# A decoder block on one core: small tables placed ahead of the large buffers in SBUF, so that the large ones start at multiples of 256 bytes

## The reference

```python
mod = c @ w_mod + b_mod;  shift, scale, gate = split(mod, 3)
u = x * (1.0 + scale) + shift
q, k, v, z_a, cb, cc, cx, z_b, g_a, g_b = split(u @ w_in)   # 8 x 1024, 2 x 2048 columns
o = rms_norm(diff_attention(rope(q), rope(k), v, lam)) * subln_gain * 0.8   # 8 heads
y_a = o * silu(z_a)
y_b = cb * causal_conv3(cc * cx, conv_w) * silu(z_b)
h = sigmoid(g_a) * (y_a @ w_proj_a) + sigmoid(g_b) * (y_b @ w_proj_b)
r = 2 ** 0.25 * x + gate * (h @ w_out)
y = layer_norm(r) * ln_gain + ln_bias
```

## Time and profile before

| | before |
|---|---|
| device time, median of 3 runs | 1579.06 us (1578.77 to 1579.44) |
| profiled execution: from its first to its last instruction (span) | 1577.2 us |
| PE matmul busy, weight load busy | 1505.7 us (95%), 1221.7 us (77%) |
| DVE, ACT, POOL busy | 820.3, 500.9, 44.0 us |
| mean granted TensorE clock | 0.989 of full speed |

### The profile page before, as it was taken

How to read it: one execution, slowest core, us unless ns; L and a number is a source line. 1 busy time by engine, 2 the same in 40 slices (tenths; PEclk the granted TensorE clock), 3 DMA queues, 4 the chain that set the end, 5 groups by cost and what they waited for, 6 DMA issues and landing times.

```text
span 1577.2 us, 18079 instructions
## 1 busy us (share of the span) xinstructions
PE 1505.7 (95%) x6600; PEld 1221.7 (77%) x6600; DVE 820.3 (52%) x1072; ACT 500.9 (32%) x693; POOL 44.0 (3%) x52
## 2 busy tenths in 40 slices
PE   2879999999999999999999999999999999999994
PEld 1657788787887878878788788888788888888883
DVE  6898773656646466463754742222523323343448
ACT  1124434325344253442434422222121221421221
POOL 0000000000000000000000000000000000000004
PEclk9999999999999999999999999999999999999997
DMA  9998333534325333243442232322232232363212
GB/s 315 348 342 249 95 106 93 156 100 116 100 62 158 106 106 106 83 129 106 118 121 92 83 133 80 106 86 100 80 107 87 99 102 84 107 243 104 106 54 107
DMA packets 215249, 200.22 MB, mean 127 GB/s; under 512 B 7730, under 2 KB 176434, under 8 KB 214450
## 3 DMA queue, kind: packets, MB, share of 16 engines
q1 hardware_dynamic: 209648, 176.52, 35.7%
q0 software_dynamic: 4608, 16.78, 3.7%
q10 hardware_dynamic: 962, 6.53, 1.0%
HBM read 195.61 MB, written 4.19 MB: 127 GB/s over the span
## 4 chain that ended last, share of the span: by engine, by line
PE 87%; DVE 6%; DMA 5%; issue 1%; ACT 1%; SPq 0%; POOLq 0%; POOL 0%; ACTq 0%; DVEq 0%
PE acc L992 27%; PE acc L994 27%; PE acc L993 27%; DMA w_mod_in<-in_w_mod 4%; PE sc L1081 2%; DVE mod_sum L631 2%; PE misc L1099 1%; DVE w_lo L604 1%; PE sc L1090 1%; DMA x_in<-in_xT 1%; DVE res L975 1%; DVE res L951 0%; DVE gate L653 0%; SPq L310 0%; DVE act_lo L658 0%
## 5 line engine op out<-in xcount | busy, mean ns | idle before, releaser
L604 DVE TENSOR_TENSOR w_lo<-raw,w_hi 128x1024 fp32r<-128x1024 f32 (+1 forms) x258 | 310.4, 1215 | 602.6 <-ACT w_hi L388 602.5
L992 PE MATMUL acc<-act_hi,w_hi 128*128 128x512 f32 x1472 | 580.6, 394 | 27.2 <-DVE w_lo L604 18.5
L994 PE MATMUL acc<-act_hi,w_lo 128*128 128x512 f32 x1472 | 576.3, 392 | 0.0
L993 PE MATMUL acc<-act_lo,w_hi 128*128 128x512 f32 x1472 | 575.8, 391 | 0.0
L388 ACT ACTIVATE w_hi<-raw 128x1024 fp32r<-128x1024 f32 (+1 forms) x258 | 268.7, 1052 | 724.2 <-PE acc L994 643.6
L992 PEld LDWEIGHTS acc<-act_hi,w_hi 128*128 128x128 f32 x1472 | 277.9, 189 | 99.3 <-issue 41.6
L994 PEld LDWEIGHTS acc<-act_hi,w_lo 128*128 128x128 f32 x1472 | 277.7, 189 | 58.5
L993 PEld LDWEIGHTS acc<-act_lo,w_hi 128*128 128x128 f32 x1472 | 278.0, 189 | 57.1 <-issue 0.2
L994 PE MATMUL acc<-y_hi,w_lo 128*128 128x512 f32 x256 | 101.0, 394 | 0.0
L993 PE MATMUL acc<-y_lo,w_hi 128*128 128x512 f32 x256 | 101.0, 394 | 0.0
L992 PE MATMUL acc<-y_hi,w_hi 128*128 128x512 f32 x256 | 101.0, 394 | 0.0
(11 more groups left out here) (151 smaller groups left out, 990.9 us busy)
## 6 DMA issues: line engine op xcount, KB each, us to landing
raw<-in_w_in SPq DMA_DIRECT2D x256, 256.0 KB
w_mod_in<-in_w_mod SPq DMA_DIRECT2D x64, 512.0 KB, 8.1
raw<-in_w_tail SPq DMA_DIRECT2D x32, 1024.0 KB
raw<-in_w_in SPq DMA_DIRECT2D x29, 1024.0 KB
gate_in<-in_w_mod POOLq DMA_DIRECT2D x32, 512.0 KB, 4.2
x_in<-in_xT SPq DMA_DIRECT2D x8, 512.0 KB, 8.9
x_tok<-in_x ACTq DMA_DIRECT2D x1, 4096.0 KB, 13.5
raw<-in_w_in SPq DMA_DIRECT2D x8, 384.0 KB
```

The source lines that it names most:

```text
L604: ins = dve.tensor_tensor(w_lo[:, f % SLOTS, :, 0:width], raw[:, (f // 2) % 2, 2 * (f % 2):2 * (f % 2) + 2, 0:width], w_hi[:, f % SLOTS, : ...
L992: pe.matmul(dst, a_hi, b_hi, start=first, stop=False)
L993: pe.matmul(dst, a_hi, b_lo, start=False, stop=False)
L994: return pe.matmul(dst, a_lo, b_hi, start=False, stop=last)
```

## The change

The small tensors are allocated first, then `raw`, the split weights and activations, `gate`, `cos` and `sin`; `gain_col`, `eps_col` and `one_col` become the three columns of one tensor `cols3`. The instructions, their order, their shapes and their waits stay as they are on all engines; only addresses differ (and the name of these columns).

```diff
-        raw = sb("raw", [P, 2, 4, COLS])
-        w_hi = sb("w_hi", [P, SLOTS, 2, COLS], F32R)
-        w_lo = sb("w_lo", [P, SLOTS, 2, COLS], F32R)
-        act_hi = sb("act_hi", [P, KT, T], F32R)
-        act_lo = sb("act_lo", [P, KT, T], F32R)
-        gate = sb("gate", [P, D])
         cst = sb("cst", [P, C_WIDTH])
-        cos = sb("cos", [P, T])
-        sin = sb("sin", [P, T])
         c_col = sb("c_col", [P, KT])
         b_col = sb("b_col", [P, 2 * KT])
         conv_col = sb("conv_col", [P, HEADS * 3])
-        gain_col = sb("gain_col", [P, 1])
-        eps_col = sb("eps_col", [P, 1])
-        one_col = sb("one_col", [P, 1])
+        cols3 = sb("cols3", [P, 3])
+        gain_col, eps_col, one_col = cols3[:, 0:1], cols3[:, 1:2], cols3[:, 2:3]
         mean_mat = sb("mean_mat", [P, P], F32R)
...
         shift_col = sb("shift_col", [P, NT])
+
+        raw = sb("raw", [P, 2, 4, COLS])
+        w_hi = sb("w_hi", [P, SLOTS, 2, COLS], F32R)
+        w_lo = sb("w_lo", [P, SLOTS, 2, COLS], F32R)
+        act_hi = sb("act_hi", [P, KT, T], F32R)
+        act_lo = sb("act_lo", [P, KT, T], F32R)
+        gate = sb("gate", [P, D])
+        cos = sb("cos", [P, T])
+        sin = sb("sin", [P, T])
```

## The result

The changed kernel takes 1563.72 us (median of 4 runs, 1563.05 to 1565.23); the kernel before took 1578.91 us beside it. The ratio is 0.9907, with a 95% interval of 0.9895 to 0.992: 15.2 us faster, where 65.1 us were forecast, and outside the range.

A forecast was written before the change was run, and what follows sets the result against it. PE was taken to bound the kernel from 160 to 1540 us by its float32r matmul pace. Gains of 67.5 + 0.5 less 2.9 us of new waits made 65.1 us: 1579.06 to 1514.0 us, range 1500 to 1545.

The forecast's parts named there:

- What tells the paces apart: Step on float32r matmuls on PE: the moving operand's start over 256 bytes, not the loaded operand, explains 226.7 against 233.4 ns.
- the unused end of a ninth block: Moving operand read in 256-byte blocks; unused elements of the last cost 32 or 48 cycles, none at rest 0: 215.5 ns.
- The 16 with sq: Matmuls in the heads with sq moving, counted with the 768 moving y: 784 x 17.9 ns = 14.0 us gain.
- The new waits in the heads: Faster PE would wait on L796 before its turns, 0.4 us per head; seven heads: -2.9 us.
- The 0.5 us of the first halves: Halves 0 to 23, in stage 1 and the first head's start: all they gain, about 0.5 us.
- The DVE term: DVE and ACT instructions on new addresses: no gain or loss; L631 with operands at rest 64 takes 747 ns.
- The few ns from the plain float32 passes: Plain float32 passes at 428 ns show about 2 ns beyond the columns, so float32r would reach 215.5 ns.
- The DMA term: Transfers landing at other SBUF addresses: nothing taken, bounds about 4 us loss or gain, 6% of 63 us on w_mod.
- A fixed 32 cycles: First rival: 544 cycles is the least for a float32r matmul with its load; only y and sq gain, 1573.8 us; chance 0.08.
- DMA gains too: Rival: landings at a rest of 0 also shorten stage 1 by 4 us, 1510 us; chance 0.05.
- Address has no say: Rival: the two matmul paces belong to something else in which y differs; 1579 us, chance 0.05.
- the slower case: Rival: a ninth block is always read, so float32r matmuls at rest 0 take 240 ns; 1649 us, chance 0.05.

## Why the prediction was wrong

**The step that failed is "What tells the paces apart".** It says that the loaded operand is no explanation, since it always has a rest of 128. But an operand that never varies cannot be excluded by that: it stood at 128 in every comparison, and what varied was as much the difference between the two rests (0 for act and w, 64 for y) as the moving rest itself. Both readings fit two points. I took the one with a mechanism that went on below 226.7, the unused end of a ninth block, and extrapolated it to a rest that no row had. The run with y at 0 and w at 128, at 233.3 ns, refutes it; the runs with all at 64 and all at 128 show the other reading.

**The terms.** With act or w moving, 4776 times 11.2 ns = 53.5 us were expected and nothing came, since their rests were equal before. With y, 784 times 17.9 ns = 14.0 us were expected; the 768 with y gained 6.7 ns each, 5.1 us, and the one layout run that undoes y's mismatch alone gives 5.0. The 16 with sq even lost a trace (701.6 for 693.1 ns over the three steps around a pair): `mean_mat` is loaded from 224 now, as unequal to sq's 0 as 32 was to 64. The new waits in the heads, -2.9 us, did not come, as nothing got faster there. The 0.5 us of the first halves is lost in stage 1's change. The DVE term, nothing, was right: L631 takes 749 ns where it took 747.

**The few ns from the plain float32 passes** were the second support, and it bore nothing: at two cycles per column they show no cost of reading at any rest (429.15 ns at 0, 64 and 128), so they could not tell whether the 32 cycles are fixed or a matter of place. Beside it stood the figure of the Trainium skill, "TensorE: Matmul & The Clock Gate", Part 1, N / 2.4 GHz + about 2.5 ns. The runs agree with it for bfloat16 (215.82 ns) and not for float32r, at any place (226.65 at the least).

**The DMA term, nothing, with bounds of 4 us either way,** was wrong as value and as bound. Stage 1 gained 8.4 us in the profiled execution, and the landings 9.3 us by the medians. Per packet the 6% that I worked the bound from was near (50.8 to 46.2 ns is 9%). What failed is what I applied it to: the 63 us of landings that stand in the chain. But the DMA engines are busy throughout the stage, so their rate sets the whole period of a group, the pieces on DVE included. Seven groups of 16.5 us at 346 GB/s are 116 us; at 383 they could be 11 us shorter, and 8.4 came through before DVE, and in two groups PE, became as long. The words that the rule is "on bytes fetched" led me to give it 0.05. That rule, the Trainium skill, "DMA: Bandwidth & Descriptors", How a descriptor splits into AXI transactions, has each unaligned start cost beats; the direction agrees with the landings here, though the fetching side never changed. Counted in its beats a rest of 128 or 192 should cost more than 64; the packets alone took 50.6, 50.4 and 50.4 ns at 64, 128 and 192 and show no such step, while their groups, each visited once, took 13.23, 13.48 and 14.07 us. The page's count is neither shown nor refuted here.

**The rivals.** "A fixed 32 cycles" (0.08) gave the right pace for y and 5.2 us, so 1573.8 us, and is what the layouts with equal rests off 256 measured: 1573.0 to 1573.5. Its reason, the handover of the load, is not what the runs show: shorter loads save nothing, and the moving element repeated takes three fifths of the cycles away. "DMA gains too" (0.05) was true as well, at twice its size, but I had coupled it only to my own forecast. Together they give 5.1 + 8.4 = 13.5 of the 13.7 us by which the span fell; neither case stood beside the other in my list. "Address has no say" and the slower case did not occur. The slower rival's direction was possible all the same, by the mismatch and not by the ninth block: the layout with act at 64 is slower than before. By the lines of 16 bytes of the Trainium skill, "SBUF — State Buffer", Door 1, nothing would have changed. The trace disagrees: all starts were at multiples of 16 bytes before and after, and the pace with y went from 233.4 to 226.7 ns.

**The signs that I named** did their work: "a pace of 226.7 for both sorts makes the first rival right" is what the timeline showed at once.

**What stays open.** Why equal rests are fast: whether a matmul shares something with its own load or with the next one (228.3 against 230.0 ns). Why the price of unequal rests is uneven: loaded 0 with moving 64 cost 228.85 ns in one kernel, 228.9 in all four visits of another and 233.35 in a third, and y in its layout had three paces by the tensors taken. The last two of these kernels allocate the same tensors in the same order, so that the places alone don't fix the price; what came before in the stream, or its length (24 or 48 matmuls), may have a part, and no run separates them. Why 384 and 256 columns show so little of it. And what the 13 cycles are that stay with the repeated element.

## What to carry to other kernels

Give all loaded and moving operands of a stream of float32r matmuls (shown for 512 columns) the same rest over 256 bytes, and start the buffers that DMAs land in at multiples of 256 bytes; a start of 0 for everything does both. Before extrapolating a fit from two rows, list what never varied in them, the partner operand first, and run or find the case that varies it alone. Rivals with causes that don't exclude each other need a case for both at once.

## What was not expected of the hardware

- The pace of a float32r matmul of 512 columns depends on two addresses together: 226.7 ns where all operands have equal rests over 256 bytes, from 226.1 up to 240.0 ns (start 20 bytes past) with unequal ones, most often 233.3 in the streams. At 384 and 256 columns hardly anything of it is seen. The Trainium skill, "TensorE: Matmul & The Clock Gate", Step-by-step, gives PE two independent read ports, one for each operand; no run shows the ports, but the two reads are not independent in time here. bfloat16 shows none of it (215.85 ns at 0, 64 and 128).
- Even at its best it takes the columns and 32 cycles, from 256 to 512 columns (448: 38), and 218.6 ns for 512 if the moving operand is one element repeated.
- Landings in rows of 1,024 bytes take 46 ns a packet from a rest of 0 with hardly a deviation, and 50 to 51 from any other that was run, for 383 against 346 GB/s in stage 1.
